# State-space batches: ScalarE swaps the halves of two products, records get shorter and lie in four buffers, the output product runs two batches behind

## The chip, the cores and the metric

The kernel runs on one core of a Trainium2 chip. A core has five engines that run side by side, each with its own in-order queue: TensorE (PE in the profile; PEld is its weight loads), VectorE (DVE), ScalarE (ACT), GpSimd (POOL) and SyncE (SP), which here only issues DMAs. They wait for one another on semaphores. The metric is the device time of one execution in microseconds, from the first to the last instruction with what the launch adds around it.

## The reference, cut to what matters

A retention layer with a feed-forward block (layer 0) is followed by a state-space mixer (`s5_mixer`), a second feed-forward block, an attention layer and a third feed-forward block. 512 tokens, width 1024, all in float32. The change touches the state-space mixer only:

```
def s5_mixer(h, w_in, lam_re, lam_im, log_step, b_re, b_im, c_re, c_im, d_skip, w_glu):
    u = (h @ w_in).reshape(bsz, seq, SSM_GROUPS, SSM_GROUP)      # 64 groups of 16 channels
    ... a_re, a_im: decay per group and state (64 states); br, bi; cr, ci
    def scan_sequence(u_seq):
        bu_re = einsum('gnk,lgk->lgn', br, u_seq)
        bu_im = einsum('gnk,lgk->lgn', bi, u_seq)
        _, _, xr, xi = associative_scan(combine, (ar_seq, ai_seq, bu_re, bu_im), axis=0)
        return einsum('gkn,lgn->lgk', cr, xr) - einsum('gkn,lgn->lgk', ci, xi)
    y = lax.map(scan_sequence, u) + d_skip * u
    z = gelu(y)
    val, gate = split(z @ w_glu, 2)
    return val * sigmoid(gate)
```

`combine` is the complex recurrence x[l] = a x[l-1] + bu[l].

## The kernel before

**Matrix products.** Every large product is three fp32r products of high and low parts (lines 358 to 360, 384 to 386, 415 to 417). Weights come in chunks of up to 128x1024 through a ring of six buffers: SyncE loads `w_raw`, ScalarE makes `w_hi` (line 1060), GpSimd makes `w_lo` (line 937). PSUM has eight banks, which are opened in rotation: `open_bank` waits until the bank opened eight openings earlier has been freed.

**Records.** While the first feed-forward block (`f1`) runs, tables for the mixer are prepared in 16 batches of 4 groups (`NB` = 16, `GB` = 4) and stored in DRAM as one record a batch, 128 partitions by `REC` = 2880 floats. In `s5_batch_out` ScalarE copies the parts into a staging buffer: `W` (what turns 8 tokens of 16 channels into a change of state; 4 groups of 128 columns and the first 64 of them a second time), `P` (4x144, what reads the state out) and `Q`, which is `P` with its upper and lower 64 partitions exchanged (lines 1125 and 1126). `M` is the part of the output that comes from the same 8 tokens; `C` and `S` are cosines and sines, 256 columns each. Partitions 0 to 63 hold real parts, 64 to 127 imaginary parts.

**The batches of the mixer.** After the input product (`u`), tokens lie as 64 columns of 8 (`NC` = 64, `T` = 8) in `u_c`. Then a loop runs over the 16 batches, written out separately for each engine:

- TensorE: `s5_states(b+1)` turns the batch's inputs (line 691; 4 transposes), `s5_inc(b)` multiplies them with `W` (line 703: 8 products, 4 for the state and 4 for the state with halves exchanged, into the two halves of one bank), `s5_out(b-1)` sums three products for each of the 4 groups (line 714: inputs by `M`; line 716: `zc` 0 by `P`; line 718: `zc` 1 by `Q`), and after every second batch `s5_turn_back` turns the result back (line 727; 8 transposes). The profile has two instructions for each of these products, and one for each transpose.
- VectorE: `z1` = bank * cos (line 1931), `z2` = exchanged half of the bank * sin (line 1932), their sum (line 1935), four scans along the columns (line 1939), the turned-back states `zc` 0 = z3 * cos (line 1947) and `zc` 1 = z3 * sin (line 1948). After every second batch it makes the low part of a finished tile (line 1464).
- ScalarE: copies the turned inputs out of PSUM (`s5_turned`, line 1293), applies gelu to the output (`s5_gelu`, line 1301), and makes the high part of a finished tile (line 1069).
- SyncE: loads record b+3 into one of three buffers, the state part (`W`, `C`, `S`; line 867) when `zc` of batch b is made, and the output part (`P`, `Q`, `M`; line 871) when the output bank of batch b is closed. The first three come by ScalarE's queue.

What follows the loop is the product with `w_glu`, whose first matmul (line 384) needs the high and low part of the last tile.

## Time and profile before

| | |
|---|---|
| median of 3 runs | 1868.02 us (1865.08 to 1869.88) |
| profiled execution | 1867.94 us |
| its span, first to last instruction | 1866.1 us |
| TensorE busy | 1794.4 us, 96% |
| VectorE busy | 810.4 us, 43% |
| ScalarE busy | 669.9 us, 36% |
| GpSimd busy | 697.9 us, 37% |
| the 16 batches, first `s5_inc` to first matmul of `w_glu` | 699.25 to 791.90, 92.65 us |

The profiled execution lies 0.08 us from the median, and 1.84 us of it lie around the span. Busy time says which engine has the most work in all; who ends a stage last is read from the stage itself: the chain of work that ended last lists, in order of time, the piece that everything behind had to wait for.

### The profile page before, as it was taken

The page shows a single profiled execution, that of the slowest core. Times are in us where ns is not written, and L with a number is a line of the kernel's source. Part 1 is how long each engine was busy: PE and PEld are TensorE (multiplying, and loading weights), DVE is VectorE, ACT ScalarE, POOL GpSimd, SP SyncE. Part 2 cuts the span into 40 slices and gives each one's busy share as a digit, 9 for nine tenths or more (in the row PEclk, how much of TensorE's full clock was granted, in tenths as well). Part 3 has the DMA queues.
Part 4 walks back from the last instruction along what each step waited for, and adds up shares of the span by engine and source line. Part 5 has one row for each costly group of instructions (what it writes and reads, how often), then busy time and mean ns, then how long its engine had stood idle before and what let it go on. Part 6 is the DMA issues. An engine that isn't in the chain of part 4 may idle for free.

```text
span 1866.1 us, 22714 instructions
## 1 busy us (share of the span) xinstructions
PE 1794.4 (96%) x9038; PEld 1503.9 (81%) x9038; DVE 810.4 (43%) x1429; ACT 669.9 (36%) x1128; POOL 697.9 (37%) x314
## 2 busy tenths in 40 slices
PE   8997989799999799999999999999999999999999
PEld 6886878588788579888988888879888898888887
DVE  4859688759957615513311011126766321110111
ACT  3432245235344642323331222246755332222221
POOL 5422235334534140042444444434540344434342
PEclk9999999899999998999999999999999999999999
DMA  9422235353544456522333333222200133332322
GB/s 240 93 68 68 57 111 166 99 165 116 176 148 154 142 192 225 200 80 80 102 101 90 102 91 102 88 76 80 94 1 1 57 113 102 91 101 80 113 85 85
DMA packets 242281, 202.21 MB, mean 108 GB/s; under 512 B 41472, under 2 KB 199296, under 8 KB 242176
## 3 DMA queue, kind: packets, MB, share of 16 engines
q1 hardware_dynamic: 238608, 192.81, 34.0%
q10 hardware_dynamic: 3568, 7.94, 1.2%
q8 instruction: 73, 1.20, 0.3%
q14 instruction: 32, 0.26, 0.0%
HBM read 175.03 MB, written 25.69 MB: 108 GB/s over the span
## 4 chain that ended last, share of the span: by engine, by line
PE 86%; DVE 9%; ACT 2%; DMA 1%; issue 1%; POOL 0%; SPq 0%; DVEq 0%; ACTq 0%
PE ps L358 13%; PE ps L360 13%; PE ps L359 13%; PE ps L384 9%; PE ps L385 9%; PE ps L386 9%; PE ps L415 2%; PE ps L417 2%; PE ps L416 2%; PE ps L703 2%; PE ps L813 2%; PE ps L794 2%; PE ps L804 1%; PE ps L714 1%; PE ps L716 1%
## 5 line engine op out<-in xcount | busy, mean ns | idle before, releaser
L937 POOL TENSOR_TENSOR w_lo<-w_raw,w_hi 128x1024 fp32r<-128x1024 f32 (+3 forms) x283 | 670.0, 2378 | 1132.3 <-ACT w_hi L1060 1132.0
L358 PE MATMUL ps<-a_hi,w_hi 128*128 128x512 f32 (+1 forms) x1184 | 443.6, 375 | 5.0 <-POOL w_lo L937 5.0
L360 PE MATMUL ps<-a_hi,w_lo 128*128 128x512 f32 (+1 forms) x1184 | 441.5, 373 | 0.0
L359 PE MATMUL ps<-a_lo,w_hi 128*128 128x512 f32 (+1 forms) x1184 | 441.4, 373 | 0.0
L1060 ACT ACTIVATE w_hi<-w_raw 128x1024 fp32r<-128x1024 f32 (+3 forms) x283 | 284.9, 1018 | 228.5 <-DMA w_raw<-in_ffn_w_gate_up_dram 72.1
L358 PEld LDWEIGHTS ps<-a_hi,w_hi 128*128 128x128 f32 x1184 | 223.7, 189 | 45.8 <-issue 7.3
L360 PEld LDWEIGHTS ps<-a_hi,w_lo 128*128 128x128 f32 x1184 | 223.7, 189 | 39.2
L359 PEld LDWEIGHTS ps<-a_lo,w_hi 128*128 128x128 f32 x1184 | 223.8, 189 | 38.7
L1991 DVE TENSOR_TENSOR ev<-ps,xh 128x512 f32<-128x512 f32 x44 | 30.4, 692 | 411.9 <-PE ps L360 382.9
L384 PE MATMUL ps<-w_hi,h_hi 128*128 128x512 f32 x476 | 189.9, 399 | 13.7 <-DVE x_rows L1530 11.4
L385 PE MATMUL ps<-w_lo,h_hi 128*128 128x512 f32 x476 | 189.0, 397 | 0.0
L386 PE MATMUL ps<-w_hi,h_lo 128*128 128x512 f32 x476 | 188.8, 397 | 0.0
L384 PE MATMUL ps<-w_hi,a_hi 128*128 128x512 f32 (+1 forms) x352 | 139.7, 397 | 12.2 <-DVE a_lo L1464 12.2
L1528 DVE TENSOR_TENSOR x_rows<-ps,x_rows 128x512 f32<-128x512 f32 x72 | 49.1, 690 | 224.6 <-PE ps L386 193.7
L385 PE MATMUL ps<-w_lo,a_hi 128*128 128x512 f32 (+1 forms) x352 | 138.2, 393 | 0.0
L386 PE MATMUL ps<-w_hi,a_lo 128*128 128x512 f32 (+1 forms) x352 | 138.0, 392 | 0.0
L384 PEld LDWEIGHTS ps<-w_hi,h_hi 128*128 128x128 f32 x476 | 90.4, 190 | 36.7 <-issue 15.3
L1076 ACT ACTIVATE h_hi<-ev 128x512 fp32r<-128x512 f32 x66 | 41.6, 630 | 212.2 <-DVE ev L1991 195.9
L386 PEld LDWEIGHTS ps<-w_hi,h_lo 128*128 128x128 f32 x476 | 90.4, 190 | 21.2
L385 PEld LDWEIGHTS ps<-w_lo,h_hi 128*128 128x128 f32 x476 | 90.4, 190 | 20.7
L384 PEld LDWEIGHTS ps<-w_hi,a_hi 128*128 128x128 f32 x352 | 68.1, 193 | 26.2 <-issue 9.7
L1166 ACT ACTIVATE xh<-ps 128x512 f32<-128x512 f32 x44 | 26.3, 598 | 165.3 <-PE ps L360 165.3
(338 smaller groups left out, 2402.9 us busy)
## 6 DMA issues: line engine op xcount, KB each, us to landing
w_raw<-in_ffn_w_gate_up_dram SPq DMA_DIRECT2D x88, 512.0 KB, 3.8
w_raw<-in_w_up_dram SPq DMA_DIRECT2D x44, 512.0 KB, 3.9
w_raw<-in_ffn_w_down_dram SPq DMA_DIRECT2D x40, 512.0 KB, 3.6
s_records<-stage SPq DMA_DIRECT2D x16, 928.0 KB, 6.1
rec<-s_records SPq DMA_DIRECT2D x13, 800.0 KB, 4.4
w_raw<-in_w_in_dram SPq DMA_DIRECT2D x20, 512.0 KB, 4.6
w_raw<-in_w_down_dram SPq DMA_DIRECT2D x20, 512.0 KB, 4.3
w_raw<-in_ssm_w_glu_dram SPq DMA_DIRECT2D x16, 512.0 KB, 3.6
```

The lines of the kernel that those rows point to most:

```text
L358: pe.matmul(bank, wh, xh_, start=first, stop=False)
L359: pe.matmul(bank, wh, xl_, start=False, stop=False)
L360: return pe.matmul(bank, wl, xh_, start=False, stop=last)
L384: pe.matmul(o, ah[:, k + kk, s], wh[:, kk, :], start=(n == 0 and kk == 0), stop=False)
L385: pe.matmul(o, ah[:, k + kk, s], wl[:, kk, :], start=False, stop=False)
L386: m = pe.matmul(o, al[:, k + kk, s], wh[:, kk, :], start=False, stop=end)
L415: pe.matmul(o, ah[:, k + kk, s], wh[:, kk, :], start=(k + kk == 0), stop=False)
L416: pe.matmul(o, ah[:, k + kk, s], wl[:, kk, :], start=False, stop=False)
L937: pool.tensor_tensor(w_lo[:, n % RING, 0:w], w_raw[:, n % RING, 0:w], w_hi[:, n % RING, 0:w].bitcast(F), ALU.subtract).then_inc(lo_made, 1)
L1060: act.activation(w_hi[:, n % RING, 0:w], w_raw[:, n % RING, 0:w], ACT.Copy).then_inc(hi_made, 1)
L1076: act.activation(hi, view(ev[:, i % 2, :]), ACT.Copy).then_inc(hi_ready, 1)
L1528: ins = v.tensor_tensor(o, b, o, ALU.add)
```

## The change

Exchanging the halves of a complex product is taken from TensorE and given to ScalarE.

- The second copy of `W` and the matrix `Q` are gone. A record has 2112 floats instead of 2880. `s5_batch_out` makes three of its six ScalarE instructions no more (lines 1125, 1126 and 1134; line 1136, a one-column copy that freed a bank, goes too), and the `W` copy frees its bank itself.
- `s5_inc` has 4 products instead of 8, `s5_out` 8 instead of 12.
- VectorE multiplies the bank with the sines into `z2`; ScalarE copies each half of `z2` to the other half of the partitions (`swap_state`, two copies of 64x256 into `sv_sw`); VectorE subtracts. After the scans, z3 * sin goes to `zs`, ScalarE exchanges its halves in the same way (`swap_scanned`, into `zs_sw`), and VectorE adds them to `zc` (`add_swapped`), which is done behind the first two products of the next batch.
- There are four record buffers instead of three, three `zc` instead of two, and four `u_t` instead of three. `s5_out` runs two batches behind `s5_inc`, and so do gelu and what follows it; two batches of it are left at the end instead of one.
- SyncE loads record b+4, its state part when `zs` of batch b is made.

```
-W_O, P_O, Q_O, M_O, C_O, S_O = 0, 768, 1344, 1856, 2368, 2624
-REC = 2880
+W_O, P_O, M_O, C_O, S_O = 0, 512, 1088, 1600, 1856
+REC, RECS = 2112, 4
...
             def s5_inc(b_):
-                for sw in range(2):
-                    for g in range(GB):
-                        o = W_O + g * 192 + 64 * sw
-                        m = pe.matmul(b[:, sw * 256 + g * NC:sw * 256 + g * NC + NC], rec[b_ % 3][:, o:o + P],
-                                      u_t[:, b_ % 3, g * NC:g * NC + NC], start=True, stop=True)
+                for g in range(GB):
+                    o = W_O + g * P
+                    m = pe.matmul(b[:, g * NC:g * NC + NC], rec[r][:, o:o + P], u_t[:, r, g * NC:g * NC + NC],
+                                  start=True, stop=True)
...
             def s5_out(b_):
-                    pe.matmul(o, zc[:, i, 0, g, :], rec[b_ % 3][:, P_O + g * 144 + GK:P_O + g * 144 + 144],
-                              start=False, stop=False)
-                    m = pe.matmul(o, zc[:, i, 1, g, :], rec[b_ % 3][:, Q_O + g * P:Q_O + g * P + P],
+                    m = pe.matmul(o, zc[:, b_ % 3, g, :], rec[r][:, P_O + g * 144 + GK:P_O + g * 144 + 144],
                                   start=False, stop=True)
...
                 s5_inc(b_)
-                if b_:
-                    s5_out(b_ - 1)
-                if b_ >= 3 and b_ % 2:
-                    s5_turn_back((b_ - 3) // 2)
+                if b_ >= 2:
+                    s5_out(b_ - 2)
+                if b_ >= 4 and b_ % 2 == 0:
+                    s5_turn_back((b_ - 4) // 2)
+            s5_out(NB - 2)
+            s5_turn_back(KT - 2)
             s5_out(NB - 1)
             s5_turn_back(KT - 1)
...
-                    for b_ in range(NB - 3):
-                        sp.wait_ge(zc_ready, b_ + 1)
-                        load_state_part(sp, b_ + 3)
+                    for b_ in range(NB - RECS):
+                        sp.wait_ge(zs_ready, b_ + 1)
+                        load_state_part(sp, b_ + RECS)
...
+            def swap_state(b_):
+                act.wait_ge(sv_turned, b_ + 1)
+                act.activation(sv_sw[0:NS, :], z2[NS:P, :], ACT.Copy).then_inc(sv_swapped, 1)
+                act.activation(sv_sw[NS:P, :], z2[0:NS, :], ACT.Copy).then_inc(sv_swapped, 1)
+
+            def swap_scanned(b_):
+                act.wait_ge(zs_ready, b_ + 1)
+                if b_:
+                    act.wait_ge(zc_ready, b_)
+                z = zs[:, :, :].rearrange("p g c -> p (g c)")
+                act.activation(zs_sw[0:NS, :], z[NS:P], ACT.Copy).then_inc(zs_swapped, 1)
+                act.activation(zs_sw[NS:P, :], z[0:NS], ACT.Copy).then_inc(zs_swapped, 1)
...
                 if b_ + 1 < NB:
                     s5_turned(b_ + 1)
+                ahead(chunks_at[("sv", b_)])
+                swap_state(b_)
+                if b_ >= 2:
+                    s5_gelu(b_ - 2)
+                if b_ >= 4 and b_ % 2 == 0:
+                    split(("zt", (b_ - 4) // 2), *turned_back((b_ - 4) // 2))
+                swap_scanned(b_)
...
+            def add_swapped(b_):
+                v.wait_ge(zs_swapped, 2 * (b_ + 1))
+                x = zc[:, b_ % 3, :, :].rearrange("p g c -> p (g c)")
+                v.tensor_tensor(x, x, zs_sw[:, :], ALU.add).then_inc(zc_ready, 1)
+                v.wait_ge(zc_ready, b_ + 1)
+
             for b_ in range(NB):
-                go(v.tensor_tensor(z1[:, :], b[:, 0:256], cs, ALU.mult))
-                r = release(("sv", b_), v.tensor_tensor(z2[:, :], b[:, 256:512], sn, ALU.mult))
-                step(v.tensor_tensor(z1[:, :], z1[:, :], z2[:, :], ALU.add))
+                v.tensor_tensor(z2[:, :], b[:, 0:256], sn, ALU.mult).then_inc(sv_turned, 1)
+                w = release(("sv", b_), v.tensor_tensor(z1[:, :], b[:, 0:256], cs, ALU.mult))
+                if b_:
+                    add_swapped(b_ - 1)
+                v.wait_ge(*w)
+                v.wait_ge(sv_swapped, 2 * (b_ + 1))
+                step(v.tensor_tensor(z1[:, :], z1[:, :], sv_sw[:, :], ALU.subtract))
```

ScalarE's queue in the middle of the loop, before: a copy of turned inputs, a gelu, and every second time a high part.

```order
L1293 ACTIVATE u_t<-ps 128x256 [waits bank_full3,bank_full1]
L1301 ACTIVATE y_c<-ps 64x8x64 [waits bank_full5]
L1293 ACTIVATE u_t<-ps 128x256 [waits bank_full6,bank_full5]
L1301 ACTIVATE y_c<-ps 64x8x64 [waits bank_full2,bank_full0]
L1069 ACTIVATE a_hi<-ps 128x8x64 [waits bank_full1]
```

The same place in the changed kernel (lines 1315 and 1316 are `swap_scanned`, 1306 and 1307 `swap_state`, 1076 is the high part):

```order
L1315 ACTIVATE zs_sw<-zs 64x256 [waits zc_ready,zs_ready]
L1316 ACTIVATE zs_sw<-zs 64x256
L1293 ACTIVATE u_t<-ps 128x256 [waits bank_full1,bank_full0]
L1306 ACTIVATE sv_sw<-z_114 64x256 [waits sv_turned]
L1307 ACTIVATE sv_sw<-z_114 64x256
L1301 ACTIVATE y_c<-ps 64x8x64 [waits bank_full3]
L1076 ACTIVATE a_hi<-ps 128x8x64 [waits bank_full4]
L1315 ACTIVATE zs_sw<-zs 64x256 [waits zc_ready,zs_ready]
L1316 ACTIVATE zs_sw<-zs 64x256
```

Four copies are new in every batch. The exchange of one batch's scanned half stands ahead of the copy of turned inputs and of the next batch's first exchange.

VectorE's queue for one batch before (`z_112`, `z_113` and `z_114` are `z1`, `z2` and `z3`; the scans stand as line 1939):

```order
L1931 TENSOR_TENSOR z_112<-ps,rec_108 128x256 [waits rec_state0,bank_full0,zc_ready]
L1932 TENSOR_TENSOR z_113<-ps,rec_108 128x256
L1935 TENSOR_TENSOR z_112<-z_112,z_113 128x256 [waits bank_free0,dve_step]
L1939 SCALAR_TENSOR_TENSOR z_114<-r_95,z_112 128x64 [waits dve_step]
L1939 SCALAR_TENSOR_TENSOR z_114<-r_95,z_112 128x64 x3
L1947 TENSOR_TENSOR zc<-z_114,rec_108 128x4x63 [waits bank_full6,dve_step]
L1948 TENSOR_TENSOR zc<-z_114,rec_108 128x4x63 [waits dve_step]
```

And now (`z_113`, `z_114` and `z_115` are `z1`, `z2` and `z3` here):

```order
L1961 TENSOR_TENSOR z_114<-ps,rec_108 128x256 [waits rec_state0,bank_full2,zs_ready]
L1962 TENSOR_TENSOR z_113<-ps,rec_108 128x256
L1953 TENSOR_TENSOR zc<-zc,zs_sw 128x256 [waits zs_swapped]
L1967 TENSOR_TENSOR z_113<-z_113,sv_sw 128x256 [waits sv_swapped,bank_free2,zc_ready]
L1971 SCALAR_TENSOR_TENSOR z_115<-r_95,z_113 128x64 [waits dve_step]
L1971 SCALAR_TENSOR_TENSOR z_115<-r_95,z_113 128x64 x3
L1979 TENSOR_TENSOR zc<-z_115,rec_108 128x4x63 [waits bank_full0,dve_step]
L1980 TENSOR_TENSOR zs<-z_115,rec_108 128x4x63 [waits dve_step]
L1484 TENSOR_TENSOR a_lo<-ps,a_hi 128x8x64 [waits hi_ready,bank_full4,zs_ready]
```

One instruction (line 1953) is new, and two waits for ScalarE stand in the middle of the batch. The low part of a tile (line 1484 now, 1464 before) stands, every second time, ahead of the next batch's first product.

## Rows read from the trace of the kernel before

**Rows 1.** From the page: busy time of each engine, share and instructions.

```profile
PE 1794.4 (96%) x9038; PEld 1503.9 (81%) x9038; DVE 810.4 (43%) x1429; ACT 669.9 (36%) x1128; POOL 697.9 (37%) x314
```

**Rows 2.** Chain in order of time (start us, us, what): one batch with its turn-back.

```profile
737.40 0.39 PE ps L691 x4
737.79 1.93 PE ps L703 x16
739.72 0.36 PE ps L714 x2
...
742.48 0.64 PE ps L727 x8
743.12 0.25 PE ps L691 x4
```

**Rows 3.** Groups of instructions from 699 to 791 us: xcount | busy us, mean ns | idle.

```profile
L1464 DVE TENSOR_TENSOR a_lo<-ps,a_hi 128x512 fp32r<-128x512 f32 x7 | 7.6, 1089 | 10.6 <-ACT a_hi L1069 10.6
L1293 ACT ACTIVATE u_t<-ps 128x256 f32<-128x256 f32 x16 | 6.2, 392 | 4.1 <-PE ps L691 4.1
L1301 ACT ACTIVATE y_c<-ps 64x512 f32<-64x512 f32 x16 | 9.5, 592 | 62.9 <-PE ps L718 62.9
```

**Rows 4.** Timeline, VectorE's work of one batch (start us, us, engine line op).

```profile
739.81 0.42 DVE L1931 TENSOR_TENSOR z<-ps,rec 128x256 f32<-128x256 f32 x1 [2.03 <-PE ps L703]
...
740.67 0.43 DVE L1935 TENSOR_TENSOR z<-z,z 128x256 f32<-128x256 f32 x1
...
742.46 0.42 DVE L1948 TENSOR_TENSOR zc<-z,rec 128x252 f32<-128x252 f32 x1
```

**Rows 5.** Groups of ScalarE from 180 to 640 us: how records are made.

```profile
L1125 ACT ACTIVATE stage<-stage 64x512 f32<-64x512 f32 x16 | 10.1, 631 | 9.9 <-DVE stage L1821 9.6
L1133 ACT ACTIVATE stage<-ps 128x512 f32<-128x512 f32 x16 | 9.4, 586 | 0.2
L1134 ACT ACTIVATE stage<-ps 128x256 f32<-128x256 f32 x16 | 5.9, 368 | 0.0
```

**Rows 6.** Waits of VectorE and of TensorE, 180 to 640 us (us in total, times, longest).

```profile
DVE stage L1816 <- DMA s_records<-stage: 2.0, 1, 2.0
...
PE ps L384 <- DVE x_rows L1530: 11.4, 1, 11.4
```

**Rows 7.** Chain in order of time, start of the loop and its end.

```profile
699.25 3.65 PE ps L703 x16
702.90 0.62 PE ps L691 x4
703.52 3.60 PE ps L703 x16
707.12 0.62 PE ps L714 x2
707.74 0.43 PE ps L716 x2
...
788.15 0.02 issue
...
791.90 0.80 PE ps L384
```

**Rows 8.** Stretches: length, busy of PE, PEld, DVE, ACT, POOL, granted clock, DMA.

```profile
699.20:709.20 10.00, 9.95 (x46) 9.62 (x47) 4.71 (x16) 1.90 (x3) 1.98 (x1) 0.50 0.23 70
709.20:784.70 75.50, 75.50 (x677) 71.11 (x675) 46.60 (x134) 18.03 (x33) 0.00 (x0) 1.00 0.71 247
...
1255.75:1257.75 2.00, 0.01 (x2) 0.04 (x1) 0.00 (x0) 1.97 (x4) 1.40 (x1) 1.00 0.11 39
...
1440.00:1443.00 3.00, 2.58 (x24) 2.44 (x23) 0.55 (x3) 1.27 (x3) 0.00 (x0) 1.00 0.01 3
```

**Rows 9.** The same columns, 1.25 us behind the gap at 1255.75.

```profile
1259.00:1260.00 1.00, 1.00 (x6) 1.00 (x5) 0.88 (x2) 0.00 (x0) 0.92 (x1) 0.50 0.06 16
```

More of the change, by code:

```diff
@@ L176, in program @@
         u_c = scratch("u_c", [NC, G, T, GK], F, 0)
-        rec = [scratch(f"rec{i}", [P, REC], F, 32 + 11.25 * i) for i in range(3)]
-        u_t = scratch("u_t", [P, 3, GB * NC], F, 66)
+        rec = [scratch(f"rec{i}", [P, REC], F, 32 + 8.25 * i) for i in range(RECS)]
+        u_t = scratch("u_t", [P, RECS, GB * NC], F, 65)
         z1 = scratch("z1", [P, GB * NC], F, 69)
@@ L181, in program @@
         z3 = scratch("z3", [P, GB * NC], F, 71)
-        zc = scratch("zc", [P, 2, 2, GB, NC], F, 72)
+        zc = scratch("zc", [P, 3, GB, NC], F, 72)
+        zs = scratch("zs", [P, GB, NC], F, 75)
+        zs_sw = scratch("zs_sw", [P, GB * NC], F, 84)
+        sv_sw = scratch("sv_sw", [P, GB * NC], F, 85)
         y_c = scratch("y_c", [NC, 2, T, P], F, 76)
@@ L247, in program @@
         u_even = sem("u_even")
+        sv_turned = sem("sv_turned")
+        sv_swapped = sem("sv_swapped")
+        zs_ready = sem("zs_ready")
+        zs_swapped = sem("zs_swapped")
         zc_ready = sem("zc_ready")
@@ L277, in program @@
         k_out = [sem(f"k_out{i}") for i in range(2)]
-        stage_w = sem("stage_w")
         e_w = sem("e_w")
         k_w = sem("k_w")
-        rec_state = [sem(f"rec_state{i}") for i in range(3)]
-        rec_out = [sem(f"rec_out{i}") for i in range(3)]
+        rec_state = [sem(f"rec_state{i}") for i in range(RECS)]
+        rec_out = [sem(f"rec_out{i}") for i in range(RECS)]
         o_out = sem("o_out")
@@ L1130, in s5_batch_out @@
                 release(("s5k", f), act.activation(k_rows(f)[:, :, KPAD:], b, ACT.Copy))
-                b = full(act, ("s5w", f)).rearrange("p (g c) -> p g c", g=GB)
-                w = stage[:, W_O:W_O + 768].rearrange("p (g c) -> p g c", g=GB)
-                act.activation(w[:, :, 0:P], b, ACT.Copy).then_inc(stage_w, 1)
-                act.activation(w[:, :, P:], b[:, :, 0:NS], ACT.Copy).then_inc(stage_w, 1)
-                act.wait_ge(stage_w, 4 * (f + 1))
-                act.activation(st[:, 189:190], eps_c[:, 0:1], ACT.Copy).then_inc(bank_free[bank_no[("s5w", f)] % 8], 1)
+                if f >= 2:
+                    act.wait_ge(st_out[f % 2], 16 * (f // 2))
+                release(("s5w", f), act.activation(stage[:, W_O:W_O + GB * P], full(act, ("s5w", f)), ACT.Copy))
             def load_second_norm():
@@ L1271, in _ @@
             act.wait_ge(e_out, 16 * NB)
-            for b_ in range(3):
+            for b_ in range(RECS):
                 load_state_part(act, b_)
@@ L1290, in s5_turned @@
             def s5_turned(b_):
[L1291 to L1293 removed]
+                if b_ >= RECS:
+                    act.wait_ge(*closed(("y", b_ - RECS)))
+                release(("ut", b_), act.activation(u_t[:, b_ % RECS, :], at(("ut", b_))[:, 0:GB * NC], ACT.Copy))
             def s5_gelu(b_):
@@ L1306, in _ @@
                     s5_turned(b_ + 1)
-                if b_:
-                    s5_gelu(b_ - 1)
-                if b_ >= 3 and b_ % 2:
-                    split(("zt", (b_ - 3) // 2), *turned_back((b_ - 3) // 2))
+                ahead(chunks_at[("sv", b_)])
[5 more added lines that the diff above has]
+                swap_scanned(b_)
+            s5_gelu(NB - 2)
+            split(("zt", KT - 2), *turned_back(KT - 2))
             s5_gelu(NB - 1)
@@ L1919, in _ @@
             split_tile("mix0", 3, to_a_s5)
-            go(v.memset(zc[:, :, :, :, 0:1], 0.0))
+            go(v.memset(zc[:, :, :, 0:1], 0.0))
+            go(v.memset(zs[:, :, 0:1], 0.0))
             settle()
@@ L1941, in _ @@
                 settle()
-                if b_ >= 2:
-                    v.wait_ge(*closed(("y", b_ - 2)))
+                if b_ >= 3:
+                    v.wait_ge(*closed(("y", b_ - 3)))
                 zv = z3[:, :].rearrange("p (g c) -> p g c", g=GB)[:, :, 0:NC - 1]
@@ L1946, in _ @@
                 sv = sn.rearrange("p (g c) -> p g c", g=GB)[:, :, 0:NC - 1]
-                step(v.tensor_tensor(zc[:, b_ % 2, 0, :, 1:], zv, cv, ALU.mult))
-                v.tensor_tensor(zc[:, b_ % 2, 1, :, 1:], zv, sv, ALU.mult).then_inc(zc_ready, 1)
-                v.wait_ge(zc_ready, b_ + 1)
-                if b_ >= 3 and b_ % 2:
-                    split(("zt", (b_ - 3) // 2), *turned_back((b_ - 3) // 2))
+                step(v.tensor_tensor(zc[:, b_ % 3, :, 1:], zv, cv, ALU.mult))
+                v.tensor_tensor(zs[:, :, 1:], zv, sv, ALU.mult).then_inc(zs_ready, 1)
+                v.wait_ge(zs_ready, b_ + 1)
+                if b_ >= 4 and b_ % 2 == 0:
+                    split(("zt", (b_ - 4) // 2), *turned_back((b_ - 4) // 2))
+            add_swapped(NB - 1)
+            split(("zt", KT - 2), *turned_back(KT - 2))
             split(("zt", KT - 1), *turned_back(KT - 1))
```

34 lines of the change are left out of this document (14 added, 20 removed).

## The prediction

> **What bounds the kernel now.** I read the page first: TensorE is busy 96% of the span [rows 1], so time is gained only where TensorE has less to do or waits less. Then the chain of work that ended last, in order of time, through the 16 batches. In their middle it stays on TensorE from one batch to the next [rows 2]: 0.39 us of transposes, 1.93 us of `s5_inc`, then `s5_out` from 739.72 to 742.48, 2.76 us. That is 5.08 us a batch; a turn-back adds 0.64 and shortens the transposes behind it to 0.25, so 5.58 us with one, 5.33 on average. The stretches say the same: from 709.2 to 784.7 us TensorE is busy all the time at the full granted clock (1.00, that is 2.4 GHz), VectorE 46.6 of 75.5 us, ScalarE 18.0 [rows 8]. ScalarE's gelu waits for TensorE 62.9 us in all [rows 3]. Work taken from TensorE is therefore gained at once, until something else ends last.
>
> At the start, from 699.2 to 709.2, the clock is 0.50 (1.2 GHz) [rows 8]; `s5_inc` takes 3.65 us there, the transposes 0.62, and a pair of matmuls of `s5_out` 0.43 [rows 7]. At the end, 3.75 us pass from the last matmul (788.15) to the first of `w_glu` (791.90).
>
> **TensorE, part by part.** `s5_inc` loses 8 of 16 matmuls: 1.93 / 2 = 0.97 us. `s5_out` keeps 16 of 24: 2.76 x 2/3 = 1.84 us. With 0.39 of transposes that is 3.20 us a batch, 3.70 with a turn-back, 3.45 on average instead of 5.33. If nothing else came in, 16 batches would give 30 us. Something does.
>
> **The new loop.** The new order gives a circle through VectorE and ScalarE. Let a batch's `zs` be ready at 0.
> - ScalarE exchanges it: two copies of 64x256. No row has that shape. The nearest are 64x512 from SBUF at 0.63 us, 128x512 from PSUM at 0.59 and 128x256 from PSUM at 0.37 [rows 5]: 256 columns less are 0.22 less, so 0.63 - 0.22 = 0.41, with 0.37 and 0.63 as bounds. Two of them and 0.09 for the signal (`s5_inc` ends at 739.72, line 1931 starts at 739.81) [rows 2, 4]: 0.93.
> - Then, in queue order, the copy of turned inputs, 0.39 [rows 3]: 1.3. `s5_inc` two batches on waits for it.
> - Then the next batch's first exchange. Its `z2` (0.42) has been made meanwhile. Two copies: 2.15, and 0.1 for the signal: 2.25.
> - VectorE's subtraction, scans and both products run as before, from the start of line 1935 to the end of line 1948: 740.67 to 742.88, 2.21 us [rows 4]. The new addition (0.42) lies in the wait before. Next `zs`: 4.45 us.
>
> Every second time VectorE first makes a low part, 1.09 us [rows 3]; then `z2` ends at 1.6, the exchange at 2.5, and the circle is 4.85 us. Gelu and the high part lie beside VectorE's 2.2 us. The mean is 4.65 us: above TensorE's 3.45, so **the circle, not TensorE, sets the pace**, and TensorE stands idle about 1.2 us a batch.
>
> **Start.** At the low clock the first `s5_inc` ends at 699.25 + 1.83 = 701.1. `z2`, exchange and VectorE's 2.21 put the first `zs` at 704.9, the next at 709.3 and 713.8. The first `s5_out` waits behind the third `s5_inc`; TensorE, still at the low clock, gets the fourth `s5_inc` done by about 714, and the fourth `zs` is there at 718.3. **Middle.** Twelve more batches, six of each kind: 12 x 4.65 = 55.8, to 774.1. **End.** Exchange 0.93, addition 0.5, `s5_out` 1.84 and a start of 0.1: 777.5. Then the same 3.75 us [rows 7]: 781.2 instead of 791.9. That is -10.7 us. The batch before, with its tile, fits ahead of it: its gelu and high part end on ScalarE before the last `s5_out` does.
>
> **Clock.** I add one spell at the low clock, 8.5 us. In it TensorE needs 0.62 + 1.83 + 8 x 0.43 = 5.9 us a batch and about 6.4 with its share of turn-backs (doubled 0.5), 1.75 more than the circle. 8.5 / 6.4 x 1.75 = +2.4 us.
>
> **Records.** ScalarE saves 0.63 + 0.63 + 0.37 + 0.20 us a batch while `f1` runs (the last, a one-column copy, has no row here). Hardly anybody waits for it: TensorE's longest wait there is for VectorE, 11.4 us, and VectorE waits 2.0 us for a store of a record [rows 6], which gets 40% shorter. Between 0 and -5 us; I take -1. The first four records are 4.3 MB where three were 4.4 MB; three more DMA issues on ScalarE lie beside the products before 690 us. Later records are loaded well over two batches ahead. A ring of eight banks with 3.5 openings a batch does not bind: the bank that `s5_inc` takes was last read two batches ago. All zero.
>
> **Sum.** -10.7 + 2.4 - 1 = -9.3: 1867.9 - 9.3 = **1858.6 us**. The profiled execution and the median of the three runs are the same to 0.1 us.
>
> **Rivals.**
> - *The clock goes up and down* (mixed, 25%). For it: at 1255.75 TensorE stood still for 2.0 us, went on, and 1.25 us later the clock was at 0.50 [rows 8, 9]. In the batches it was at 0.50 for 10 us though TensorE was busy 9.95 of them, mostly with line 703, and came back 2 us after `s5_out` began [rows 7, 8]. The new loop has a gap of 1.2 us and less `s5_out` in each batch. Against it: from 1440 to 1443 us, with 0.42 us of gaps in 3, it held [rows 8]; the gaps of the new loop are shorter than 2.0 us. With half of the batches at the low clock, 12 x 0.5 x 1.75 = +10.5 instead of +2.4: **1866.7 us**, the same as before. The same time comes out if an exchange copy costs 0.63 and not 0.41: four a batch, 12 x 0.88 = +10.6.
> - *The clock stays low* (10%), the slower side. Its place is the start: the first two batches have no `s5_out`, and TensorE waits between them. If it never comes back before the end, 12 batches take 6.4 us, not 4.65: +21, and the last `s5_out` 1.6 more. 1867.9 - 10.7 + 21 + 1.6 - 1 = **1879 us**. It is slower than before as soon as more than about half of the batches run so.
> - *ScalarE is no obstacle* (10%): copies overlap, exchanges take 0.37 and start at once. VectorE alone takes about 4.1 us a batch, and record making gives 3 us: -10.7 - 6.6 - 3 = -20; **1848 us**.
> - *It doesn't do what it says* (5%): a bank or a record comes late and each batch stays at 5.3: about -3, then +3 at the longer end: **1868 us**.
>
> The Trainium skill, "TensorE: Matmul & The Clock Gate", in "HAM oscillation — how this bites in real kernels" and "A second HAM failure mode: psum-queue depth-cycling", says that short idle spells between groups of matmuls can make the clock go up and down. By that page this change, which puts such a spell in each batch, is in danger; the gap at 1255.75 agrees with it, the stretch at 1440 does not. By the page the second case above (1866.7) would be the likelier. The same skill, "ScalarE: Activation LUTs", "What ACT_TABLE_LOAD costs", gives 186 ns and 0.833 ns a column for such a copy, and an overlap of 93 ns: an estimate of 0.40 us, and 0.31 for each that overlaps. By it the circle would be about 0.3 us shorter and the sum 1855.
>
> **Chances.** Forecast 50%, up and down 25%, low 10%, no obstacle 10%, not as said 5%. A measurement of this kernel can tell about 0.3%, 5.6 us. Faster by more (below 1862.3): nearly all of the forecast, all of the fourth case, a fifth of the second: 0.60. Within: 0.27. Slower: 0.13. The range reaches from the fast case to a little over the mixed one, 1848 to 1874.
>
> **What would show it.** Lines 1967 and 1953 on VectorE waiting for ScalarE; exchange copies of 0.4 us, back to back with the copy of turned inputs; `zs` every 4.45 or 4.85 us; TensorE idle about 1.2 us before each `s5_inc`, waiting for ScalarE's copy; `s5_inc` 0.97 us at the full clock; 3.75 us at the end. A granted clock near 0.95 from 710 to 780 us confirms the forecast, 0.75 the second case, 0.5 the third. The sum is wrong if a pair of copies takes over 1.2 us, or if the clock is what decides.

## The result, and the profile after

The changed kernel takes **1848.28 us**, the median of 4 runs (1848.04 to 1852.99), beside 1867.13 us for the kernel before in 4 runs on the same chip. The ratio is 0.9908, with a 95% interval from 0.9887 to 0.9930. The forecast was a gain of 9.3 us; 18.9 were measured. The time lies at the lower end of the range, and the sign was right.

Three more comparisons of the same two kernels, made with the experiments, gave 0.9929 [0.9907, 0.9952], 0.9928 [0.9914, 0.9942], and in single runs 1848.28 beside 1866.7 us. So the gain is between 14 and 19 us; the two comparisons with the most runs have the 14.

Busy time of each engine, from the page of the changed kernel (busy us, share of the span, instructions), to be read beside [rows 1]:

```profile
PE 1769.5 (96%) x8782; PEld 1477.9 (80%) x8782; DVE 820.1 (44%) x1446; ACT 668.8 (36%) x1128; POOL 698.1 (38%) x314
```

TensorE has 24.9 us less to do and VectorE 9.7 more. The span falls by 19.4, from 1866.1 to 1846.7 us.

The chain of work in order of time (start us, us, engine, tile, line), one batch in the middle of the new loop. It answers to [rows 2]:

```profile
742.43 0.43 DVE zs L1980
742.88 0.03 ACT zs_sw L1315
...
743.76 0.38 ACT u_t L1293
...
744.17 0.07 ACT sv_sw L1306
...
744.61 0.42 ACT sv_sw L1307
...
745.16 0.44 DVE z L1967
...
745.83 0.64 DVE z L1971 x3
746.49 0.43 DVE zc L1979
746.94 0.43 DVE zs L1980
```

TensorE has gone from the chain. What ends last goes from `zs` (line 1980) to ScalarE's exchange of it, to the copy of turned inputs, to the exchange of the next batch's `z2`, back to VectorE's subtraction (line 1967), the scans and the next `zs`: 746.94 - 742.43 = 4.51 us. That is the circle of the forecast, piece by piece.

ScalarE in the same batch, from its timeline (start us, us, engine, line, operation, tiles, count):

```profile
742.88 0.42 ACT L1315 ACTIVATE zs_sw<-zs 64x256 f32<-64x256 f32 x1 [1.75 <-DVE zs L1980]
743.32 0.42 ACT L1316 ACTIVATE zs_sw<-zs 64x256 f32<-64x256 f32 x1
...
744.17 0.41 ACT L1306 ACTIVATE sv_sw<-z 64x256 f32<-64x256 f32 x1
...
745.05 0.59 ACT L1301 ACTIVATE y_c<-ps 64x512 f32<-64x512 f32 x1
745.54 1.08 ACT L1076 ACTIVATE a_hi<-ps 128x512 fp32r<-128x512 f32 x1
```

An exchange copy takes 0.41 to 0.42 us and the next starts 0.44 us behind it. The high part starts 0.49 us behind a gelu of 0.59 us. Waits from 699 to 778 us (engine, line, waited for: us in total, times, longest):

```profile
ACT zs_sw L1315 <- DVE zs L1980: 22.1, 16, 2.4
DVE z L1967 <- ACT sv_sw L1307: 11.4, 16, 1.0
...
PE ps L708 <- issue: 7.7, 9, 1.9
```

VectorE and ScalarE wait for each other in all 16 batches. For TensorE's wait before `s5_inc` the profile names no releaser; in the batch above its `s5_inc` starts at 744.25, 0.11 us behind the end of the copy of turned inputs (743.76 + 0.38). Where the clock stays at 1.00 this wait is 1.16 and 0.81 us in turn (`again`, 724 to 747 us), about 1.0 on average. The end of the loop in the chain, beside [rows 7]:

```profile
769.97 0.43 DVE zs L1980
...
771.38 0.43 DVE zc L1953
...
771.86 0.43 PE ps L719 x2
...
773.60 0.23 PE ps L721 x2
773.86 0.60 ACT y_c L1301
...
774.50 0.72 PE ps L730 x8
775.24 1.09 ACT a_hi L1076
...
776.43 1.10 DVE a_lo L1484
...
777.58 0.79 PE ps L390
```

From 773.83 to 777.58 are the same 3.75 us as before. From the first `s5_inc` (696.20) to the first matmul of `w_glu` (777.58) this execution takes 81.4 us, where before it was 791.9 - 699.25 = 92.6: -11.2 us. I call this stretch the stage below. Stretches of it (length, busy of PE, PEld, DVE, ACT, POOL, granted clock, DMA share, GB/s), beside [rows 8]:

```profile
699.00:709.00 10.00, 8.08 (x39) 7.35 (x39) 6.97 (x21) 5.05 (x13) 0.00 (x0) 0.50 0.17 55
...
720.00:730.00 10.00, 8.80 (x66) 7.91 (x64) 8.28 (x22) 7.04 (x16) 0.00 (x0) 0.83 0.67 224
730.00:740.00 10.00, 8.78 (x65) 7.96 (x65) 8.28 (x25) 6.88 (x15) 0.00 (x0) 0.83 0.65 217
740.00:750.00 10.00, 8.42 (x75) 7.66 (x75) 7.92 (x23) 7.03 (x16) 0.00 (x0) 1.00 0.81 267
750.00:760.00 10.00, 9.59 (x74) 8.77 (x73) 8.24 (x25) 6.56 (x14) 0.00 (x0) 0.83 0.65 219
760.00:770.00 10.00, 8.22 (x60) 7.30 (x59) 8.21 (x25) 5.87 (x12) 0.00 (x0) 0.83 0.02 8
```

The clock does go up and down here: four of the five stretches from 720 us on have 3.4 us at 1.2 GHz in them (10 x 0.17 / 0.5), and the granted clock is 0.90 over the whole from 709 to 777.5. Yet from the start of one batch's scans to the next it is 4.51 us, or 4.65 to 4.68 with a low part, in stretches of either kind. A second profile of the same kernel (`again`) has two such spells where this one has four (granted clock 0.94 from 712.8 to 775), and its 16 batches take the same 81.4 us.

### The profile page after: what moved, and what is told of

Same layout as the page of the kernel before. It is cut to its first block, busy times and chain, and to the rows that moved or that the text cites. A ratio compares the mean times of both kernels' runs of the same rounds, so it can differ in the third digit from the quotient of the medians.

```text
span 1846.7 us, 22249 instructions
## 1 busy us (share of the span) xinstructions
PE 1769.5 (96%) x8782; PEld 1477.9 (80%) x8782; DVE 820.1 (44%) x1446; ACT 668.8 (36%) x1128; POOL 698.1 (38%) x314
## 3 DMA queue, kind: packets, MB, share of 16 engines
q8 instruction: 71, 1.16, 0.3%
## 4 chain that ended last, share of the span: by engine, by line
PE 83%; DVE 10%; ACT 3%; issue 2%; DMA 1%; POOL 0%; DVEq 0%; SPq 0%; ACTq 0%
PE ps L364 13%; PE ps L366 13%; PE ps L365 13%; PE ps L390 10%; PE ps L391 9%; PE ps L392 9%; PE ps L421 2%; PE ps L423 2%; PE ps L422 2%; PE ps L818 2%; PE ps L799 2%; PE ps L809 1%; PE ps L791 1%; PE ps L644 1%; DVE z L1971 1%
```

## The experiments

All are edits of the changed kernel, except where the text says so. "The stage" and "behind it" (from the first matmul of `w_glu` to the end) are read from each profiled execution, as is the distance between batches, from scans to scans. Each ratio is against the kernel before, on the same chip. Where two distances stand, the second is that of a batch with a low part or a turn-back; the first batches of the loop, in which the clock is low, can differ. The table has the numbers; the sections read them.

| kernel | median us | ratio [95%] | between batches us | stage us | behind it us |
|---|---|---|---|---|---|
| changed, `again` | 1853.35 | 0.9929 [0.9907, 0.9952] | 4.51 / 4.67 | 81.45 | 1069.3 |
| changed, `again2` | 1851.93 | 0.9928 [0.9914, 0.9942] | 4.51 / 4.67 | 81.43 | 1069.6 |
| changed, `again3` | 1848.28, one run | | 4.51 / 4.67 | 81.42 | 1069.2 |
| `e1_copy_more` | 1858.65 | 0.9962 [0.9948, 0.9976] | 4.81 / 4.97 | 87.42 | 1073.0 |
| `e2_product_more` | 1856.29 | 0.9945 [0.9926, 0.9964] | 4.51 / 4.67 | 82.82 | 1071.8 |
| `e8_record_copies` | 1853.22 | 0.9927 [0.9908, 0.9947] | 4.51 / 4.67 | 81.38 | 1069.3 |
| `e3_order` | 1848.96 | 0.9902 [0.9879, 0.9926] | 4.12 / 4.35 | 77.01 | 1072.5 |
| `e6_glu_early` | 1849.94 | 0.9907 [0.9886, 0.9929] | 4.51 / 4.67 | 74.2 | 1072.9 |
| `e9_order_early` | 1845.65 | 0.9894 [0.9880, 0.9909] | 4.12 / 4.35 | 71.26 | 1072.8 |
| `e4_out_only` | 1863.22 | 0.9981 [0.9965, 0.9997] | 4.2 to 6.3 | 90.26 | 1070.7 |
| `e5_state_only` | 1860.86 | 0.9962 [0.9944, 0.9980] | 3.65 to 6.8 | 88.51 | 1069.0 |
| `e10_out_four` | 1852.13 | 0.9930 [0.9911, 0.9949] | 4.21 / 4.70 | 81.17 | 1069.7 |
| `e11_three_buffers` | 1854.88 | 0.9952 [0.9936, 0.9969] | 4.51 / 4.67 | 82.42 | 1073.9 |
| before, `before_b` | 1865.27, one run | | 5.09 / 5.57 | 92.7 | 1072.9 |
| before, `before_c` | 1865.75, one run | | 5.09 / 5.57 | 92.5 | 1072.1 |
| before, `before_d` | 1869.04, one run | | 5.09 / 5.57 | 94.05 | 1072.8 |

### Is it the circle: a copy more, or a product more

`again` is the changed kernel unedited. 

> The changed kernel itself, a second time. In its first profile the 16 batches (first s5_inc to first matmul of w_glu) took 81.40 us against 92.65 before, and 8.1 us more were gained outside them, of which about 4.5 where the granted clock did not fall (near 893, 1259 and 1348 us of the kernel before). Theory: the batches are the steady part and come out at 81 to 82 us again, with zs every 4.51 or 4.66 us; the rest of the gain is mostly the luck of where the clock falls, so that the ratio to the kernel before lies between 0.990 and 0.994. Rival: all of it belongs to the change, and the ratio is 0.990 again, with the same clock outside the batches.

`e1_copy_more` makes ScalarE do one of the exchange copies twice in each batch, into a tile that nobody reads:

```diff
                 act.wait_ge(sv_turned, b_ + 1)
+                act.activation(spare[0:NS, :], z2[NS:P, :], ACT.Copy)
                 act.activation(sv_sw[0:NS, :], z2[NS:P, :], ACT.Copy).then_inc(sv_swapped, 1)
```

> ScalarE makes one copy of 64x256 more in each batch, into a spare tile, ahead of the exchange of the state: 0.42 to 0.44 us more in the circle of VectorE and ScalarE. Theory (the circle sets the pace): zs every 4.95 and 5.1 us, 16 x 0.44 = 7.0 us more than the changed kernel, 1855 us. Rival (TensorE or its clock sets the pace): no more than 1 us.

`e2_product_more` makes TensorE do 8 matmuls of `s5_out` twice in each batch, which is the work it lost there:

```diff
+                    pe.matmul(o, u_t[:, r, g * NC:g * NC + NC], rec[r][:, M_O + g * P:M_O + g * P + P],
+                              start=True, stop=True)
                     pe.matmul(o, u_t[:, r, g * NC:g * NC + NC], rec[r][:, M_O + g * P:M_O + g * P + P],
                               start=True, stop=False)
```

> s5_out makes the product with M twice for each group, the first for nothing: 8 matmuls and 0.86 us more of TensorE in each batch at the full clock, 4.3 in all of a batch of 4.6. Theory (TensorE has room): the middle stays at 4.51 and 4.66 us, 1 us more at the end of the loop, 1849 to 1850 us. If the spells at the low clock cost time, a fuller TensorE has fewer of them and the kernel is not slower at all. Rival (TensorE is close to the bound): 14 x 0.86 = 12 us more.

Measured: the copy makes every batch 0.30 us longer, of either kind (4.81 and 4.97), and the stage 6.0 us. The product, 8 x 0.11 us on TensorE, leaves the batches at 4.51 and 4.67, but for one of 5.14 us; the stage grows by 1.4 us, 0.9 of it at the end, where the last `s5_out` is on the chain. So the circle sets the pace and TensorE has room. The median of `e2` is 2.9 us above `again`, more than the 1 us expected; its profile has 2.5 us more behind the stage, for which see the last of these sections. ScalarE's timeline with the extra copy shows how it came to cost 0.30 and not 0.44:

```profile
742.10 0.41 ACT L1307 ACTIVATE spare<-z 64x256 f32<-64x256 f32 x1
742.42 0.40 ACT L1308 ACTIVATE sv_sw<-z 64x256 f32<-64x256 f32 x1
742.84 0.41 ACT L1309 ACTIVATE sv_sw<-z 64x256 f32<-64x256 f32 x1
```

Behind the extra copy, which signals nobody, the next starts after 0.32 us, before it has ended; behind the copy that signals VectorE, after 0.42. That the signal makes the difference is not shown: the gelu at 745.05 above signals TensorE, and the next instruction starts 0.10 us before its end all the same.

### What each part of the change is worth

`e4_out_only` keeps the second matrix of `s5_inc` and moves the output product two batches behind, with the exchange of the scanned half and, as before, three record buffers:

```diff
-REC, RECS = 2112, 4
+REC, RECS, UTS = 2368, 3, 4
...
+                for sw in range(2):
+                    for g in range(GB):
+                        o = W_O + g * 192 + 64 * sw
...
-                ahead(chunks_at[("sv", b_)])
-                swap_state(b_)
```

> One part alone: only the output's exchange is ScalarE's. s5_inc makes its 8 products with the doubled W, as before the change; Q is gone. Three record buffers of 2368 floats. TensorE has 4.2 us a batch and 4.7 with a turn-back at the full clock, 4.4 on average; VectorE and ScalarE's circle is shorter (the exchange of the state, 0.85 and two signals, is gone): about 3.7 us, 4.3 with a low part. Theory: TensorE bounds again, 4.4 us a batch instead of 4.59, so 3 us less in the middle, 1 us less at the start (no exchange in the first batch) and as much at the end as now: 1845 us. Rival (the gain needs both parts): 1855 us or more.

`e5_state_only` does the reverse: the state's halves are exchanged by ScalarE, and `s5_out` keeps its third matrix, with three record buffers:

```diff
-REC, RECS = 2112, 4
+REC, RECS, UTS = 2624, 3, 4
...
+                    pe.matmul(o, zc[:, b_ % 3, g, :], rec[r][:, P_O + g * 144 + GK:P_O + g * 144 + 144],
+                              start=False, stop=False)
+                    m = pe.matmul(o, zs[b_ % 3][:, g, :], rec[r][:, Q_O + g * P:Q_O + g * P + P],
...
-                swap_scanned(b_)
```

> The other part alone: only the state's exchange is ScalarE's. s5_out makes its 12 products with Q, which is made and stored as before the change. Three record buffers of 2624 floats. TensorE 4.37 us a batch on average; the circle is z2, exchange, subtraction to zs: 0.45 + 1.05 + 2.3 = 3.8 us, 4.9 with a low part ahead of it, 4.35 on average, and no exchange at the end of the loop. Theory: 4.5 us a batch, 1 us less at the end: 1846 us. Rival (both are needed): 1855 us or more.

Both came out irregular and missed what was expected (1845 and 1846 us): alone, with three buffers, the parts give 4 and 6 us. TensorE's waits in the stage have a row that neither kernel of the comparison has, first with the output product alone:

```profile
PE ps L709 <- DMA rec<-s_records: 4.2, 6, 1.6
```

and with the exchanged state alone:

```profile
PE ps L707 <- DMA rec<-s_records: 7.7, 8, 1.7
```

In the chain of the first, one batch reads so:

```profile
738.90 5.71 DMA rec<-s_records
...
744.66 2.00 PE ps L709 x16
746.66 0.36 PE ps L720 x2
747.02 0.32 PE ps L722 x2
747.34 0.43 PE ps L720 x2
```

A record comes late; behind the gap TensorE falls to the low clock, where a pair of `s5_out` takes 0.43 instead of 0.22 us; the batch ends later, and so does the next transfer, which waits for it. That raised a question: is it the buffers, or TensorE's load. Two kernels answer it. `e10_out_four` is `e4_out_only` with a fourth record buffer:

```diff
-REC, RECS, UTS = 2368, 3, 4
+REC, RECS, UTS = 2368, 4, 4
```

> The output product two batches behind with the second matrix kept (as in the experiment with the output product alone), but with four record buffers of the long record instead of three. With three, TensorE waited for record transfers 4.2 to 5.3 us in all and the batches came every 4.2 to 6.3 us, 90.3 us for the stage. If those waits were what made it irregular, the batches now come every 4.4 us or so (TensorE's own work in a batch of 24 matmuls more), the stage takes 78 to 82 us and the kernel about 1850 us, level with the changed kernel: the exchange of halves by ScalarE would then be worth nothing that a fourth buffer doesn't give. If TensorE's clock is the cause (a batch that is nearly all TensorE, and a fall of the granted clock that costs there at once), periods of 5 to 6 us stay around each spell of the low clock and the stage takes 86 to 90 us: about 1857 us.

`e11_three_buffers` is the changed kernel with three:

```diff
-REC, RECS = 2112, 4
+REC, RECS, UTS = 2112, 3, 4
```

> The changed kernel with three record buffers instead of four, all else as it is. The record of a batch is freed by its output product, which is now two batches behind, so that a transfer can start only when the batch before the one it is for has nearly been begun. If the fourth buffer is what lets the circle run at its own pace, some batches wait for their record: periods of 5 us and more, the stage 84 to 90 us, 1855 to 1860 us. If the shorter record arrives in time all the same, nothing changes: periods of 4.51 and 4.67 us, a stage of 81.4 us, 1851 us.

With four buffers the batches are regular, 4.21 us and 4.70 with a turn-back once the start (one of 5.83 us) is over, the stage is 81.17 us, and the time that of `again2`, run beside it: 1852.13 and 1851.93 us. The chain shows that this is TensorE's own pace, 0.39 + 1.93 + 1.90 = 4.22 us:

```profile
746.11 0.39 PE ps L697 x4
746.50 1.93 PE ps L709 x16
748.42 0.36 PE ps L720 x2
...
750.10 0.22 PE ps L722 x2
750.31 0.64 PE ps L731 x8
```

So the exchange of the state's halves by ScalarE adds nothing to the time of the other parts as the change has it: it takes 0.97 us of TensorE's work away and puts two copies of 0.44 us into the circle, and the two loops end level. Its room shows only with a better order on ScalarE, below: there the circle (4.24 us on average) gets under TensorE's 4.45 of this loop. `s5_out` without its third matrix, two batches behind, *with the fourth buffer*, is enough for the whole gain. Whether the exchanged state with a fourth buffer would be enough too was not run: by the forecast's pieces TensorE would have 0.39 + 0.97 + 2.76 = 4.12 us a batch there and 4.62 with a turn-back, an estimate that is level with the 4.21 and 4.70 of `e10`. No run has `s5_out` one batch behind either. With three of the short records the changed kernel itself loses only 1.0 us in the stage, all of it in one batch of 5.65 us, less than the 84 to 90 us expected of it; TensorE waits for records there too (7.0 us in all), mostly inside the circle's slack:

```profile
PE ps L708 <- DMA rec<-s_records: 7.0, 7, 1.7
```

`e8_record_copies` gives ScalarE back the three copies of each record that the change removed (two of 64x512, one of 128x256; the one-column copy stays out), into spare tiles:

```diff
+                act.activation(q[0:NS], c1[NS:P], ACT.Copy).then_inc(act_step, 1)
+                act.activation(q[NS:P], c1[0:NS], ACT.Copy).then_inc(act_step, 1)
...
+                act.activation(spare_w[:, :].rearrange("p (g c) -> p g c", g=GB), b[:, :, 0:NS], ACT.Copy)\
+                   .then_inc(act_step, 1)
```

> While the records are made, ScalarE again makes the copies that the change removed (two of 64x512, one of 128x256, into spare tiles; 1.63 us a batch), but the records stay short. Theory (3 us were gained ahead of the batches, by ScalarE's copies or by the clock near 270 us): if the copies are it, the first s5_inc comes 2 us later than in the changed kernel, 1850 us; if it is the clock or the shorter stores, it comes at the same time within 1 us and the time is 1848.

1853.22 us beside 1853.35 for `again`: those copies cost nothing that can be measured where they stand. In the profiles the first `s5_inc` comes at 701.3 and 699.8 us, but kernels with the same code ahead of it as the changed one have 695.8 to 701.9 there. What the shorter stores of the records are worth no run shows.

### Shortening the circle and the end

`e3_order` lets ScalarE make the exchange of `z2` ahead of the copy of turned inputs and of the exchange of the batch before's `zs`; VectorE's addition and low part move with it:

```diff
-                if b_ + 1 < NB:
-                    s5_turned(b_ + 1)
                 ahead(chunks_at[("sv", b_)])
                 swap_state(b_)
+                if b_ + 1 < NB:
+                    s5_turned(b_ + 1)
+                if b_:
+                    swap_scanned(b_ - 1)
...
-                swap_scanned(b_)
```

> The same work in another order. ScalarE: exchange of the state first, then the copy of turned inputs, then the exchange of the batch before. VectorE: the low part stands in the wait for the state's exchange, the addition behind the scans. The circle: 0.45 + 0.09 + 0.87 + 0.1 + subtraction, scans, addition and two products 2.75 = 4.25 us, and 4.4 with a low part (1.09 in a wait of 1.0). Theory: 4.33 instead of 4.59 a batch, 15 x 0.26 = 4 us less, 1844 us. Rival (the order does not matter, TensorE's clock does): 1848 us.

The batches come every 4.12 and 4.35 us, the stage is 77.0: 4.4 us less, where 4 were expected. Behind it 3 us are lost again (1072.5), so that the median, 1848.96 us, is not clearly under those of the changed kernel in other comparisons. On ScalarE the second copy of the exchange is now followed by the copy of turned inputs, which no longer stands between VectorE and its subtraction:

```profile
740.96 0.41 ACT L1307 ACTIVATE sv_sw<-z 64x256 f32<-64x256 f32 x1
741.40 0.38 ACT L1293 ACTIVATE u_t<-ps 128x256 f32<-128x256 f32 x1
```

`e6_glu_early` lets the glu product begin on the tiles that are ready, and puts the last batch's `s5_out` and turn-back in between:

```diff
+            def last_batch(n):
+                if n == 3:
+                    s5_out(NB - 1)
+                    s5_turn_back(KT - 1)
+
+            rows_product(("glu_g", 0), ssm_w_glu_2[0], a_hi, a_lo, KT, D, HALF, 2,
+                         wait_k=lambda k: zt_first + k + 1, between=last_batch)
```

> The changed kernel, with the first product of w_glu started before the last batch is through: its first three chunks (tiles 0 to 5) stand ahead of the last batch's s5_out and turn-back. In the changed kernel TensorE is idle or nearly so for 5.9 of the last 7.6 us, 5.3 us of them with nothing at all in its queue. 72 matmuls of 0.23 us are 16 us at the full clock. Theory: the end of the loop is covered by them: 5 to 8 us less, 1842 us. Rival (the first chunk waits for its tiles as long, or the last batch is late and TensorE waits behind): within 2 us of 1848.

The first matmul of `w_glu` comes 7.2 us earlier, counted from the first `s5_inc`. The last `s5_out` with its turn-back, 2.5 us, now lies behind it, so 4.7 us are saved there; behind it the profiled execution takes 1072.9 us, and the median is 1849.9. Against the runs of the changed kernel in other comparisons (1848.3 to 1853.4) that is no gain I can call measured, where 5 to 8 us were expected.

`e9_order_early` has both edits. As in `e3_order`, the exchange of the state stands first on ScalarE, ahead of the copy of turned inputs. 

> The changed kernel with two edits that were each tried alone: ScalarE makes the turned copies for the next batch ahead of the swapped copies of this one (alone: batches every 4.12 and 4.35 us, 77.0 us from the first state product to the glu product instead of 81.4), and the glu product's first columns are begun before the last batch has been put out (alone: 74.2 us to the first glu matmul, about 3.4 us off the whole). Theory that the circle between VectorE and ScalarE sets the batches: both gains add up in the loop, with the first glu matmul about 70 us after the first state product; of the early start no more than 3 us is kept, since the glu product later waits for its own weights. By that 1851.3 - 4.4 - 2 = about 1845 us. Rival, that what the early start saves is given back whole where the weights are late: 1847 us, as the order alone.

1845.65 us, beside 1851.93 for the changed kernel on the same chip; the intervals, 0.9880 to 0.9909 and 0.9914 to 0.9942, do not meet. It beats both kernels, by 6 and by 20 us. Its stage is 71.3 us, 1.5 above what the two savings alone make together (81.4 - 4.4 - 7.2 = 69.8); why is not shown.

### Where the rest of the gain lies

The stage accounts for 11.2 us of 18.9. For the rest I ran the changed kernel twice more and the kernel before three times, for their profiles.

> The changed kernel once more, beside the others of this call. Circle theory: the stage at 81.4 us, periods 4.51 and 4.67. What lies outside the stage is not set by the edits: the time is 1848 to 1854 us, by where in the rest of the kernel the granted clock falls.

> The changed kernel once more, for its profile, on the same chip as the three of the kernel before: a stage of 81.4 us with batches every 4.51 and 4.67 us wherever the clock falls in it, a remainder of 1069 to 1073 us.

> The kernel before once more, for its profile alone. The profile of the kernel before that the forecast was made from has 92.6 us from the first state product to the glu product, the granted clock at 1.00 in all but its first 10 us, and 1074.2 us behind it; the changed kernels have 81.4 us and 1069.0 to 1073.9 us. Theory that the rest of the difference is where the clock falls: other executions of the kernel before have the same 92.6 us within 0.5 us or more where a spell of the low clock lies in the batches, and their remainder spreads as that of the changed kernels does, 1069 to 1075 us. Rival, that the edits change something behind the stage: the remainder is 1074 us every time.

> As before_b, one more execution: a stage of 92 to 95 us, a remainder anywhere from 1069 to 1075 us if it is the clock's falls, at 1074 us if it is the edits.

> As before_b, one more execution: a stage of 92 to 95 us, a remainder anywhere from 1069 to 1075 us if it is the clock's falls, at 1074 us if it is the edits.

Means of four profiles of each kernel, with those at the top of this document: spans 1865.2 and 1847.7 us, 17.5 less. The stage is 93.0 and 81.4 (-11.6), what lies ahead of it 699.2 and 697.0 (-2.2; from 697.9 to 700.4, and from 695.9 to 699.8), and what lies behind it 1073.0 and 1069.3 (-3.7). The code behind the stage is the same in both. What differs there is the granted clock. Two places in which TensorE stands still, for 2.0 and for 1.7 us, are found in every execution, some 463 and 550 us behind the start of the glu product. In `before_b`, the first two rows are the first place and 1.4 us later, the last two the second place (the columns as above):

```profile
1252.60:1254.60 2.00, 0.55 (x5) 0.32 (x3) 0.32 (x1) 1.94 (x5) 1.01 (x1) 1.00 0.32 120
1256.00:1258.00 2.00, 2.00 (x10) 2.00 (x9) 1.27 (x2) 0.37 (x1) 1.30 (x1) 0.50 0.04 8
1340.60:1342.60 2.00, 0.96 (x4) 0.38 (x2) 2.00 (x10) 1.72 (x3) 1.92 (x3) 1.00 0.90 329
1344.00:1346.00 2.00, 2.00 (x8) 1.29 (x7) 1.04 (x4) 1.74 (x8) 1.92 (x2) 0.50 0.00 0
```

The same places in `again3`:

```profile
1239.30:1241.30 2.00, 0.58 (x5) 0.34 (x3) 0.35 (x1) 1.94 (x5) 0.99 (x1) 1.00 0.36 134
1242.70:1244.70 2.00, 2.00 (x17) 2.00 (x16) 1.29 (x2) 0.40 (x1) 1.35 (x1) 1.00 0.03 8
1325.80:1327.80 2.00, 0.47 (x3) 0.19 (x1) 1.97 (x9) 1.94 (x5) 1.92 (x3) 1.00 1.01 373
1329.20:1331.20 2.00, 2.00 (x12) 1.29 (x11) 1.75 (x7) 1.82 (x8) 1.92 (x2) 1.00 0.00 0
```

The gaps are alike: TensorE is idle for 1.98 to 1.99 us at the first and for 1.73 to 1.74 at the second in all eight profiles. In `before_b`, the clock is at 0.50 behind the first and the second; in `again3` it stays at 1.00 behind both, and 17 matmuls go through in the time of 10. A third place is the start of the glu product itself: 3 us at the low clock in the changed kernel, 6 in two of the four profiles of the kernel before. (It is the spell near 791 us of the first profile; at 893, which the expectation of `again` names, the clock is at 1.00.) Summed over the profile, but for the last 3 us of the span, the time at the low clock behind the stage orders the remainders of all the kernels that start the glu product in the same way:

| at the low clock behind the stage, us | kernels | behind the stage, us |
|---|---|---|
| 13.0, 12.5 | before (first profile), e11 | 1074.2, 1073.9 |
| 11.1, 10.2, 10.2, 10.2 | e1, before_b, before_d, e3 | 1073.0, 1072.9, 1072.8, 1072.5 |
| 9.6, 9.0 | before_c, e2 | 1072.1, 1071.8 |
| 6.8 | e4 | 1070.7 |
| 2.9 to 3.4 | changed (4 profiles), e5, e8, e10 | 1069.0 to 1069.7 |

A microsecond at the low clock costs about half a microsecond (5.2 us over 10). The first place had a fall in 4 of 4 profiles of the kernel before and in none of 4 of the changed kernel, the second in 3 of 4 and in none. Edits that touch nothing behind the stage bring falls back: one copy more per batch (`e1`), the other order (`e3`) and three buffers (`e11`) both, the doubled product (`e2`) the first alone. So this part of the gain is real for this pair of kernels, but it hangs on where the clock falls and not on work that the change saves. What decides whether the same gap brings a fall is open.

## Why the prediction was right or wrong

- **What bounds the kernel, TensorE's part, the circle: right.** 4.51 us a batch where 4.45 was worked out, 4.67 where 4.85 was, a mean of 4.59 against 4.65. `e1` and `e2` show it: 0.3 us on ScalarE moves every batch, 0.9 us on TensorE none but one.
- **The copy of 64x256: right.** 0.41 to 0.42 us where the estimate from the nearest rows gave 0.41 [rows 5]. Two of them and the signal, forecast at 0.93 us, take 0.99 (744.17 to 745.16). The page "ScalarE: Activation LUTs" of the Trainium skill, section "What ACT_TABLE_LOAD costs", gives figures from which 0.40 is an estimate for a copy and 0.31 for one that overlaps; the trace agrees with the first, and with the second only behind the extra copy of `e1` (0.32), while the exchange copies of the change start 0.44 us apart.
- **Start, middle and end: right.** 81.95 us from 699.25 to 781.2 in the forecast, 81.4 measured; the term -10.7 was -11.2, or -11.6 by the means. The 3.75 us at the end stayed to the hundredth.
- **Clock, +2.4: wrong.** This is the first term that failed (its own product, 8.5 / 6.4 x 1.75, is 2.3). The spells came, and more than the one I priced: four in the stage beside the start. They cost nothing: the stage is 81.4 us with four of them and with two (`again`). I took a spell to make a batch as long as TensorE's 6.4 us in it, over 8.5 us; the spells are 3.4 us long, shorter than a batch. What follows is worked out, no run tests it by itself: in such a one TensorE loses about half of it, 1.7 us at most and less where it is idle anyway, and it has about 1.0 us of idle time in each batch to take that up. Where the slack is gone the same spell does cost: in `e4` pairs of `s5_out` at 0.43 us stand on the chain.
- **Records, -1: not borne out.** `e8` gives ScalarE's copies back and loses nothing; the shorter stores, the other part of the term, were not tried.
- **Rest of the kernel, 0: wrong, and the largest miss.** I let all that lies outside the stage stay as in the one profile of before. That profile had the most time at the low clock behind the stage of all that I have (13.0 us), and the changed kernel has 3.3. By the means this is -3.7 behind the stage, and -2.2 ahead of it, where the spread within a kernel (2.5 and 3.9 us) is as large as the difference, so that I don't claim it; with the five edits whose code ahead of the stage is the changed kernel's (`e1`, `e2`, `e3`, `e6`, `e9`) its mean there is 698.5, and the difference 0.7. In the first comparison all of it fell one way: -11.2, -3.1 ahead and -5.1 behind make the 19.4 us of the two spans, where the sum had -10.7 + 2.4 in the stage, -1 ahead of it and 0 behind. The 5 us behind the stage hang on where the clock falls: by so much the size of the measured gain is luck.
- **The rival of the clock that goes up and down: it happened, and its price was wrong.** The clock at 0.90 lies nearer to the 0.95 that I gave the forecast than to the 0.75 of this case; but the ups and downs are there, and the time did not follow. The Trainium skill, "TensorE: Matmul & The Clock Gate", "A second HAM failure mode: psum-queue depth-cycling", says that short idle spells between groups of matmuls make the clock go up and down and cost throughput. The clock agrees in part: with idle spells of up to 1.16 us in each batch the changed kernel has two to four falls in the loop behind its start, `e2`, where TensorE is busy 53.8 of 55 us, has none, but neither have `e3` and `e9`, whose loops have idle spells too, each of 0.57 us or less up to 762 us. That it costs throughput holds in these runs only where TensorE is what ends last. The case that the clock stays low did not come.
- **The fastest rival, 1848 us, hit the number for another reason.** It wanted VectorE alone to set the pace, at 4.1 us a batch. Only `e3` comes near that pace (4.12 and 4.35), by another order on ScalarE. That the time lay inside the range is luck in this sense. The measured 1848.28 us came from 4.59 us a batch and a kinder clock elsewhere.
- **What the change is good for** was not asked of the forecast, and the runs show it: `s5_out` two batches behind with one matrix less and the fourth buffer are enough for the gain, and the exchanged state beside them is level with the second matrix.

## What to carry to other kernels

Where work is taken from the engine that bounds a loop, follow the new dependencies once round with the durations of the nearest rows: the circle here came out within 0.06 us on the common batch, and it also says which copy to move next (`e3`, 4.4 us in the loop). A step that is put a batch later can need a buffer more for what it reads (9 us between `e4` and `e10`, 1 between the changed kernel and `e11`); try the parts of such a change with the buffers they need, or their sum can't be read from them. Take more than one profile of the kernel before: a granted clock that falls in gaps far from the edit moved the whole by 4 to 5 us here, a fifth to a quarter of the gain.

## What the runs showed of the hardware that I had not expected

- The same gap of 2 us of TensorE, in the same code, was followed by 3.4 us at 1.2 GHz in 4 of 4 profiles of one kernel and in none of 4 of the other.
- Copies on ScalarE of 64x256 started 0.42 to 0.44 us apart in the exchanges, without overlap, and 0.32 apart behind the extra copy of `e1`; other instructions of the same queue overlap by 0.10 us. What decides it is open.
- With its idle time in pieces of 0.57 us or less (`e3`, `e9`, up to 762 us) TensorE had no fall of the clock in the loop behind its start; with pieces of 1.16 us, and about as much idle time in all (busy 84% against 82% in `e3`), it had two to four.
- Three buffers with a transfer of 4.3 to 5.8 us in the chain, against batches of 4.2 us, made periods of 4.2 to 6.3 us: a late record, the clock's fall behind the gap, and a later start of the next transfer went round together.
